# Delta rule of a linear-attention block: decay rows by one small product and a broadcast through memory, the sign and the unit diagonal of A folded into other steps

## What is computed

```python
g = -jnp.exp(A_log) * jax.nn.softplus(a + dt_bias)
g_cum = jnp.cumsum(to_chunks(g), axis=-1)
decay = jnp.exp(jnp.where(causal, g_cum[..., :, None] - g_cum[..., None, :], -jnp.inf))
k_beta = kc * bc[..., None]
m = jnp.where(strict, jnp.einsum('bhnid,bhnjd->bhnij', k_beta, kc) * decay, 0.0)
a_mat = m + jnp.eye(C)
uw = lax.linalg.triangular_solve(a_mat, rhs, left_side=True, lower=True, unit_diagonal=True)
attn_intra = jnp.einsum('bhnid,bhnjd->bhnij', qc, kc) * decay
```

## Time and profile before

| | |
|---|---|
| median of 3 runs | 902.82 us (902.63 to 904.8) |
| profiled execution | 903.8 us, of which the span is 901.5 us |
| TensorE busy | 889.5 us, 99% of the span |
| VectorE busy | 614.0 us, 68% |
| ScalarE busy | 460.0 us, 51% |
| GpSimd busy | 89.6 us, 10% |
| chain that ended last | PE 77%, DVE 15%, ACT 5%, issue 2%, DMA 1% |

### The profile page before, as it was taken

The page is one execution under the profiler, slowest core; times in us unless marked ns, Lnnn a source line. Parts: engine busy times, 40 slices in busy tenths (PEclk is TensorE's granted clock), DMA queues, the critical chain, the costliest instruction groups (busy, mean ns, idle before and its releaser), DMA issues.

```text
span 901.5 us, 12792 instructions
## 1 busy us (share of the span) xinstructions
PE 889.5 (99%) x5442; PEld 762.2 (85%) x5442; DVE 614.0 (68%) x735; ACT 460.0 (51%) x560; POOL 89.6 (10%) x94
## 2 busy tenths in 40 slices
PE   8999999999999999999999999999999999999997
PEld 8989888788888887888888888888888888888885
DVE  5999886776566557777858665666567566664665
ACT  6775554554444447555444365443355555444543
POOL 2041231100000000000124210110100000000000
PEclk9999999999999999999999999999999999999999
DMA  9754315146555543654564544354544456445531
GB/s 331 269 189 172 109 56 190 69 164 242 197 194 195 198 186 141 222 187 146 204 218 180 186 157 170 141 187 187 185 188 144 157 189 232 173 180 211 187 140 47
DMA packets 26089, 160.45 MB, mean 178 GB/s; under 512 B 3577, under 2 KB 4233, under 8 KB 8241
## 3 DMA queue, kind: packets, MB, share of 16 engines
q1 hardware_dynamic: 23616, 153.40, 46.6%
q0 software_dynamic: 2272, 6.24, 2.1%
q10 hardware_dynamic: 144, 0.00, 0.0%
HBM read 158.57 MB, written 2.63 MB: 179 GB/s over the span
## 4 chain that ended last, share of the span: by engine, by line
PE 77%; DVE 15%; ACT 5%; issue 2%; DMA 1%; POOL 0%; SPq 0%; POOLq 0%; DVEq 0%; ACTq 0%
PE banks L503 32%; PE banks L471 19%; PE banks L474 10%; DVE t_wl L1637 6%; PE banks L575 3%; PE banks L531 2%; ACT t_wh L1143 2%; PE banks L426 2%; DVE t_cout L1666 2%; PE banks L414 1%; PE banks L445 1%; PE banks L767 1%; PE banks L971 1%; DVE t_cv L1666 1%; DMA t_cout<-in_xT 1%
## 5 line engine op out<-in xcount | busy, mean ns | idle before, releaser
L1637 DVE TENSOR_TENSOR t_wl<-t_raw,t_wh 128x2048 fp32r<-128x2048 f32 x136 | 312.5, 2319 | 109.3 <-ACT t_wh L1143 108.2
L471 PE MATMUL banks<-t_hx,t_wh 128*128 128x512 f32 x992 | 312.1, 396 | 0.2 <-DVE t_wl L1637 0.2
L1143 ACT CAST t_wh<-t_raw 128x2048 fp32r<-128x2048 f32 x136 | 255.8, 1907 | 12.6 <-DMA t_raw<-in_W 7.9
L474 PEld LDWEIGHTS banks<-t_hx,t_wl 128*128 128x128 f32 x992 | 186.3, 188 | 43.7
L474 PE MATMUL banks<-t_hx,t_wl 128*128 128x256 f32 x992 | 194.9, 278 | 0.0
L471 PEld LDWEIGHTS banks<-t_hx,t_wh 128*128 128x128 f32 x992 | 153.3, 189 | 2.7 <-DVE t_wl L1637 0.4
L503 PE MATMUL banks<-t_wh,t_hx 128*128 128x512 f32 x320 | 101.6, 394 | 0.0
L503 PEld LDWEIGHTS banks<-t_wh,t_hx 128*128 128x128 f32 x320 | 59.5, 188 | 12.5 <-issue 0.3
L503 PE MATMUL banks<-t_wl,t_hx 128*128 128x512 f32 x160 | 61.1, 390 | 0.0
L2284 POOL TENSOR_TENSOR t_st<-t_st,t_half 128x1 f32<-128x1 f32 (+1 forms) x18 | 10.6, 589 | 435.5 <-DVE t_st L1666 426.1
L1475 ACT COPY t_hold<-banks 128x512 f32<-128x512 f32 x28 | 16.4, 585 | 65.3 <-PE banks L474 54.6
(11 more groups left out here) (331 smaller groups left out, 1349.9 us busy)
## 6 DMA issues: line engine op xcount, KB each, us to landing
t_raw<-in_W SPq DMA_DIRECT2D x139, 1024.0 KB, 4.8
t_raw<-in_W SPq DMA_DIRECT2D x8, 256.0 KB, 6.2
t_raw<-in_W SPq DMA_DIRECT2D x4, 512.0 KB, 8.8
skew<-scr POOLq DMA_DIRECT2D x1, 1536.0 KB, 13.8
t_cout<-in_xT SPq DMA_DIRECT2D x4, 256.0 KB, 5.4
t_x<-in_x SPq DMA_DIRECT2D x2, 512.0 KB, 10.1
t_tab<-in_tab POOLq DMA_DIRECT2D x1, 640.0 KB, 7.6
out<-t_xt SPq DMA_DIRECT2D x2, 320.0 KB, 2.3
```

What stands on the lines that cost most here:

```text
L471: e.matmul(bank[b + c], M.wh[:, h, wk], M.hx[:, k, :, :].rearrange("p a s -> p (a s)"), start=k == 0, stop=False)
L474: m = e.matmul(bank[b + c][:, 0:S], M.wl[:, h, wk], M.hh[:, k, :], start=False, stop=k == 7)
L1143: e.copy(M.wh[:, h, :], M.raw[:, r, :]).then_inc(q.sem, q.tick(("hi", i)))
L1637: e.tensor_tensor(M.wl[:, h, :], M.raw[:, r, :], M.wh[:, h, :].bitcast(F32), ALU.subtract).then_inc(q.sem, q.tick(("lo", i)))
```

## The change

- The 16 products that repeat the rows on all partitions (L672, 16 instructions, each printed as two passes) become one product of `graw` (16 columns) with the triangular matrix, `("rows")`, which gives 16 rows of 128 in PSUM bank 0. ScalarE copies them to SBUF (`grow`, placed before the three SiLUs of conv step 3), GpSimd stores them to a DRAM buffer `gscr` (8 KB), waits, and loads them back with a step of zero over the partitions into `dU` (1 MB in SBUF). Both are placed in GpSimd's list after the issue of `skew` and ahead of the four loads from it.
- The 16 subtract-and-cap instructions of VectorE now read `dU` in SBUF instead of PSUM, and move from the end of conv step 3 to conv step 5, between `rn1` and the `next_unit()` behind it; VectorE waits there for the landing of `dU`.
- The step `dS` (one instruction over 128 x 2048) goes. `("AT", g)` multiplies the products of keys with `dU` directly. The minus sign is put on the transposed keys by ScalarE's copy (scale -1), the mask and the unit matrix come from one maximum with a table that has 1 on the diagonal and -1e30 everywhere else, where `A` had an addition. Since `kq`'s keys now carry the sign, the right-hand side `r1` adds where it subtracted.

```diff
-    parts = [(i <= j).astype(np.float32), -(i < j).astype(np.float32), np.ones((128, 128), np.float32),
+    parts = [(i <= j).astype(np.float32), np.where(i == j, 1, NEG).astype(np.float32), np.ones((128, 128), np.float32),
...
+            M.grow = M.va[0:16, 0, 128:256]
...   tensor, after conv unit 3
-                    for g in range(4):
-                        b = take(("decay", g), g)
-                        opened(b)
-                        for i in range(4):
-                            s = 4 * g + i
-                            m = e.matmul(bank[b][:, i * 128:i * 128 + 128],
-                                         M.graw[:, s:s + 1].broadcast_to([128, 128]), M.triu, start=True, stop=True)
-                        m.then_inc(q.sem, q.tick(("decay", g)))
-                        drain(b, DV, ("dU", g))
+                    b = take("rows", 0)
+                    opened(b)
+                    e.matmul(bank[b][0:16, 0:128], M.graw, M.triu, start=True, stop=True).then_inc(
+                        q.sem, q.tick("rows"))
+                    drain(b, AC, "grow")
...   scalar
                 if u == 3:
+                    q.wait_ge(PE, "rows")
+                    e.copy(M.grow, bank[at["rows"]][0:16, 0:128]).then_inc(q.sem, q.tick("grow"))
                     silu_of(0)
...
-            q.wait_ge(DV, ("dU", 3))
+            q.wait_ge(DV, "dU")
             e.activation(M.dU[:], M.dU[:], ACT.Exp).then_inc(q.sem, q.tick("dexp"))
...
-                    e.copy(dst, quarters(bank[at["kT", c, w]][:])).then_inc(q.sem, q.tick(("kT", c, w)))
+                    e.activation(dst, quarters(bank[at["kT", c, w]][:]), ACT.Copy,
+                                 scale=-1.0 if w == 1 else 1.0).then_inc(q.sem, q.tick(("kT", c, w)))
...   vector, conv step 5
                     ts(rk, rk, EPS, None, ALU.add, None, "rn1")
+                    q.wait_dma(LD["dU"])
+                    for s in range(16):
+                        stt(M.dU[:, s, :], M.dU[:, s, :], M.gcum[:, s:s + 1], M.cap, ALU.subtract, ALU.min, "dU")
                     next_unit()
...   vector, conv step 3
-                    for g in range(4):
-                        b = at["decay", g]
-                        q.wait_ge(PE, ("decay", g))
-                        for i in range(4):
-                            s = 4 * g + i
-                            stt(M.dU[:, s, :], bank[b][:, i * 128:i * 128 + 128], M.gcum[:, s:s + 1], M.cap,
-                                ALU.subtract, ALU.min, ("dU", g))
...
-            q.wait_ge(AC, "dexp")
-            tt(M.AT, M.dU[:], rep(M.nstrict, 16), ALU.mult, "dS")
...
-                q.wait_ge(q, "dS")
-                tt(a_, v[:, :, 0, :], a_, ALU.mult, ("AT", g))
+                q.wait_ge(AC, "dexp")
+                tt(a_, v[:, :, 0, :], du, ALU.mult, ("AT", g))
...
-            tt(M.AT, M.AT, rep(ident[:], 16), ALU.add, "A")
+            tt(M.AT, M.AT, rep(M.unit_or_low, 16), ALU.max, "A")
...
-                    tt(M.r1, M.tm[:, 1, 1024:1536], M.r1, ALU.subtract, "r1")
+                    tt(M.r1, M.tm[:, 1, 1024:1536], M.r1, ALU.add, "r1")
...   gpsimd, after the issue of skew
+            q.wait_ge(AC, "grow")
+            e.dma_start(A["gscr"], M.grow).then_inc(LD["gscr"], 16)
+            q.wait_dma(LD["gscr"])
+            e.dma_start(M.dU[:], bass.AP(A["gscr"].tensor, 0, [[0, 128], [128, 16], [1, 128]])).then_inc(LD["dU"], 16)
             load_T(0)
             load_T(1)
             q.wait_ge(DV, "rn1")
...
+    A["gscr"] = nc.dram_tensor("gscr", [16, 128], F32, kind="Internal").ap()
```

More of the change, by code:

```diff
@@ L282, in memory @@
         M.kd = tm[:, 0, 0:512]
-        M.triu, M.nstrict, M.ones, M.near, M.same, delta, M.cap = (tab[:, i, :] for i in range(7))
+        M.triu, M.unit_or_low, M.ones, M.near, M.same, delta, M.cap = (tab[:, i, :] for i in range(7))
         M.delta = delta[:, 0:BASE]
@@ L368, in build @@
         LD = {n: top.enter_context(nc.semaphore("in_" + n)) for n in (
-            "x0", "x1", "small", "ident", "tab", "onehot", "neg", "rbT", "scr", "skew", "post_mix", "post_mlp",
+            "x0", "x1", "small", "ident", "tab", "onehot", "neg", "rbT", "scr", "skew", "gscr", "dU", "post_mix", "post_mlp",
             "dist", "rope", "g_final", "pre", "wab", *(f"T{h}" for h in range(8)), *(f"xT{p}" for p in range(4)),
```

## The result

| | before | changed |
|---|---|---|
| median | 903.65 us (15 runs) | 905.53 us (15 runs) |
| ratio to before | | 1.0016, 95% interval 1.0009 to 1.0023 |
| profiled execution | 903.8 us, span 901.5 us | 905.35 us, span 903.2 us |
| TensorE busy | 889.5 us | 885.9 us |
| VectorE busy | 614.0 us | 611.4 us |

The change makes the kernel about 1.5 us slower (0.16%), less than the 0.3% that the prediction set as its bound for "same", but on the slower side beyond the interval. The forecast was 0.8 us. TensorE is busy for 3.6 us less, and none of it is gained.

A forecast was written before the change was run, and what follows sets the result against it. VectorE's list was taken to carry the chain until the key transposes at 70.27 us. Removed from the chain 0, added waits 0.5 + 0.3 = 0.8 us: median 902.8 becomes 903.6 us, own range 901.7 to 905.0, with rivals 901.2 to 907.0.

The forecast's parts named there:

- What bounds the kernel: Up to the key transposes at 70.27 us VectorE's list carries the chain; TensorE work removed before then is worth 0.
- Rival B: Removed decay products ahead of unit 4: TensorE's 3.4 us come through, giving 899.4 us; chance 0.08.
- `dS` and the signs: VectorE's 2.28 us `dS` at 70.60 is hidden by TensorE's work; removal worth 0, same-shape replacements 0.
- The two waits: VectorE waits 0.5 us for the cast of unit 6 and 0.2 to 0.3 us for TensorE at `scaled(5)`; 0.8 us.
- conv 5: At `scaled(5)` VectorE arrives at 49.7 us, TensorE's unit is done at 49.9; a wait of 0.2 to 0.3 us.
- The source in SBUF: The 16 subtract-and-cap instructions on VectorE cost the same from SBUF as from PSUM; range -1.1 to +1.1 us.
- The landing of `dU`: GpSimd's transfers: `gscr` lands at 46.2, 1 MB takes 7.8 us, `dU` lands at 54.0; costs nothing.
- The margin of 1.2 us: Time between the landing of `dU` at 54.0 us and VectorE asking for it at 55.2.
- rival A: `dU` lands late at 58.8 us, VectorE waits 3.6 us, 4.4 in all, 907.2 us; chance 0.22.
- a cover: TensorE's 2.3 us wait for "lo" ahead of unit 4 hides the small product's 0.22 us.

The follow-up runs named there:

- e3: Kernel before with one of the 16 decay products on TensorE, VectorE's list unchanged; 904.66 us against 904.04, ratio 1.0008.
- e2: Kernel before with only the signed key copies, the maximum and no `dS`; 903.74 us against 904.04, ratio 0.9996.
- e10: Changed kernel with the decay rows' transfer ahead of `skew` and GpSimd's roots ahead of the loads from `skew`; 905.56 us against 903.7, ratio 1.0016.
- e11: Changed kernel with eight unread products of a constant in TensorE's pause ahead of unit 4; 904.39 us against 903.7, ratio 1.0004.
- e1: Changed kernel keeping rows and transfer, with `dS`, the added unit matrix and unsigned key copies of before; 905.71 us against 904.04, ratio 1.0013.
- e5: Changed kernel with the 1 MB load of `dU` issued twice, VectorE waiting for the second; 910.83 us against 903.81, ratio 1.007.
- e6: Changed kernel with the 16 subtract-and-cap instructions and the exponents moved later, off the key transposes' path; 904.33 us against 903.81, ratio 1.0004.
- e7: e6 with ScalarE's cast of unit 11 moved ahead of the token copies and the exponent; 902.66 us against 903.81, ratio 0.9985.
- e12: e7 with eight unread products in TensorE's pause ahead of unit 4; 901.34 us against 903.7, ratio 0.9969.
- e8: e7 with the decay rows' store and load ahead of the issue of `skew`; 911.0 us against 903.81, ratio 1.0082.
- e4: Changed kernel with the decay rows' store and load ahead of the issue of `skew` in GpSimd's list; 906.39 us against 904.04, ratio 1.0022.
- e9: e8 with GpSimd's roots ahead of the four loads from `skew`; 902.65 us against 903.7, ratio 0.998.

## Why the prediction was right or wrong

**What bounds the kernel: right.** VectorE's list carries the chain until the key transposes. e3 shows it without the change: 3.3 us of TensorE removed, VectorE's rows unmoved, nothing gained. Rival B is refuted. Unit 4 began behind its "lo" as forecast, 2.3 us behind the start of the products.

**`dS` and the signs: right.** Worth nothing (e2, +0.01 us in the stretch).

**The two waits: right in mechanism, the second too large.** The cast was waited for 0.51 us, forecast 0.5. For conv 5 0.2 to 0.3 us were forecast; at full clock there is hardly a wait (0.07 us). With small pieces the sum is 0.65 us (e10, e11), forecast 0.8. The median of e11, which is the change without the two things I missed, is 0.69 us above before.

**The source in SBUF: right.** 4.29 us against 4.22; the Trainium skill's table (VectorE: DVE Perf Modes, the TRN2 errata) gives a lower fixed cost for SBUF, and this trace doesn't show it for instructions with two inputs in SBUF.

**The landing of `dU`: the value was wrong, the price right.** The step took 46.2 for the landing of `gscr`, "since most of its 4.8 us can pass while `skew` ends". It landed at 49.67, 8.17 us after its issue. In part the whole execution was 1.0 us late and `skew` itself was issued 1.8 us later; in part `skew` took 15.2 us instead of 13.8. The store landed 0.6 us behind it, and in all seven traces with this order (changed, e1, e5, e6, e7, e11, e12) it landed 0.2 to 0.7 us behind `skew`: it is `skew` that sets this time, as the step had it, and the step had `skew` too early. The 1 MB then took 6.7 us, forecast 7.8. The margin of 1.2 us was gone and 0.57 us of rival A came true in this execution; in e1 and e11 the landing was in time (the store 4.9 and 5.0 us). e5 shows the price: 4.4 us more of wait made 4.4 us more of stretch, before what the clock added.

**What is missing in the sum: TensorE's pause is not free.** The prediction names the wait for "lo" as a cover ("inside the 2.3 us for which TensorE waits for "lo" anyway") and calls work removed under it worth 0. It is worth less than 0: before, the 16 products kept TensorE busy until the "lo" came; without them it idles for 1.9 us, and then some executions run at 1.2 GHz for about 3.4 us. The unit that VectorE waits for arrives 1.4 to 1.5 us later. VectorE already waits 0.07 us for TensorE at that place at full clock, so nothing is to spare and the loss is paid. Between e10 and e11 it is 1.2 us in the median, the larger part of what the change costs.

The Trainium skill (TensorE: Matmul & The Clock Gate, Part 1) describes a clock that depends on recent activity and so a pause as a possible cost. The page speaks of longer pauses than this one. The traces agree that the clock falls with a pause, and show it for 1.9 us too, in four of ten.

What stays open: for the timed executions only the mean clock of the whole program is known and not where it fell, so that most of them are at half clock in this place is argued from the medians, the mean clocks and the two groups of e6's and e10's times. And e10 and e11 differ in the two exchanges besides the products; the changed kernel and e11, which differ in the products alone, stand 1.88 and 0.69 us above the medians of before that were measured with them.

**The forecast in all.** 903.6 us against before's 902.8 was +0.8; the measured ratio gives +1.5, within the forecast's own range. The median itself, 905.53, is above that range's 905.0, since before's median of 15 runs is 903.65 and not the 902.82 of three that the range was built on. Of the 1.5 us, 0.65 are the waits that were forecast, and a further 0.9 are, as far as e11 tells, the clock and the landing, for which the sum had nothing; that they were small enough for the range is luck.

## What to carry to other kernels

Work that is hidden under a wait can still do something: here the products on TensorE that ended just as its data arrived kept its clock up, so before taking such work away ask what the engine does in the gap, and fill it if an engine waits for what comes behind; here a gap of 1.9 us mattered, and eight idle products in it gave back 1.2 us. A transfer through memory costs little time but needs a place in two lists: one in the queue, where a small store landed after 1.6 us alone and after up to 8.2 us behind a 1.5 MB transfer, and one in the issuing engine, where everything behind its wait moves too. The gain of moving a value from PSUM to SBUF was not the cheaper product but the freedom to use it later: only when the 16 instructions and the exponent left the chain, a cast of ScalarE went ahead of them and the gap was filled (e12) did the change pay its full 2.4 us.

## What the runs showed of the hardware

The granted clock of TensorE fell to half with pauses of 1.9 us (in four of ten traces), of 4.85 us (e8) and of 6.01 us (e5's for the second landing). With the short pause it fell when the pause ended (e5, between 35.5 and 36 us, the pause ending at 35.72) or 0.6 to 1.3 us later, when matmuls ran again (e1, e3, e4), and stayed at 0.50 for about 3.4 us. In the long ones it fell while TensorE still stood: at about 66.1 us in e5 (the pause ends at 67.56) and 69.7 us in e8 (72.00), and it stayed at 0.50 until 73.0 and 79.5 us. It stood at 1.00 behind the changed kernel's pauses of 1.62 and 1.55 us and behind the one of 0.96 us in e10.

GpSimd's two roots over 128 x 16, the same instructions everywhere, took 7.88 us before, 9.74 in the changed kernel and 5.92 in e9. The Trainium skill (SBUF — State Buffer, who interferes with whom) says that an instruction of VectorE with both inputs in SBUF contends with GpSimd's reads of SBUF. The 16 subtract-and-cap instructions are of this kind in the changed kernel, but they are not what made the roots longer. In e5 the first root runs while VectorE stands, and the second wholly beside the 16, from 61.02 us on (timelines of GpSimd from 55 to 60.5 us and from 60 to 64 us):

```profile
58.55 2.93 POOL L2278 TENSOR_TENSOR t_gs<-t_gs,t_half 128x16 f32<-128x16 f32 x1
61.46 2.92 POOL L2278 TENSOR_TENSOR t_gs<-t_gs,t_half 128x16 f32<-128x16 f32 x1
```

In the changed kernel, too, the first root, which ran beside these 16, took 2.91 us; the second, 6.83 us, ran on beside the "lo" of unit 8 and the last taps, which also have both inputs in SBUF. In e9 the first root ran beside that "lo" and took 2.91 us. So what makes a root longer stays open; nobody waited for the roots in the changed kernel and in e9.
